# A feed-forward inner tile turned by VectorE in 32x32 blocks and put in order through DRAM, where TensorE turned it

## What is computed

```python
D_FF = ((8 * D_MODEL // 3 + 255) // 256) * 256     # 5632

def swiglu_ffn(x, norm_pre, w_gate, w_up, w_down, norm_post):
    h = rms_norm(x, norm_pre)
    a = jax.nn.silu(jnp.einsum('bsd,df->bsf', h, w_gate)) * jnp.einsum('bsd,df->bsf', h, w_up)
    y = jnp.einsum('bsf,fd->bsd', a, w_down)
    return x + rms_norm(y, norm_post)
```

## Time and profile before

| | us |
|---|---|
| median of 3 runs (lowest, highest) | 2074.62 (2074.54, 2075.27) |
| the profiled execution's own time | 2073.36 |
| its span | 2071.6 |
| TensorE busy within the span | 2033.2 |
| VectorE, ScalarE, GpSimd busy | 1181.7, 987.6, 197.6 |
| mean granted TensorE clock | 0.994 |

### The profile page before, as it was taken

How to read it: one execution, slowest core, us unless ns; L and a number is a source line. 1 busy time by engine, 2 the same in 40 slices (tenths; PEclk the granted TensorE clock), 3 DMA queues, 4 the chain that set the end, 5 groups by cost and what they waited for, 6 DMA issues and landing times.

```text
span 2071.6 us, 28886 instructions
## 1 busy us (share of the span) xinstructions
PE 2033.2 (98%) x10074; PEld 1724.3 (83%) x10074; DVE 1181.7 (57%) x1449; ACT 987.6 (48%) x1165; POOL 197.6 (10%) x118
## 2 busy tenths in 40 slices
PE   8999999999999999999999979999999999999998
PEld 6798888888888888888899968888888888888886
DVE  5745565555555544444599996565555555544444
ACT  5544464544455443433744475454444444443433
POOL 0000000000000000000688640000000000000000
PEclk9999999999999999999999989999999999999999
DMA  7735565555555555555355415565555555555554
GB/s 242 252 128 188 176 213 190 188 188 192 191 186 190 187 188 194 193 194 193 136 187 182 159 62 168 167 217 190 192 189 187 191 185 190 192 189 193 194 194 144
DMA packets 105128, 382.31 MB, mean 185 GB/s; under 512 B 11682, under 2 KB 12066, under 8 KB 104546
## 3 DMA queue, kind: packets, MB, share of 16 engines
q1 hardware_dynamic: 103968, 375.58, 54.3%
q0 software_dynamic: 944, 5.51, 0.8%
q10 hardware_dynamic: 148, 0.27, 0.1%
HBM read 379.21 MB, written 2.10 MB: 184 GB/s over the span
## 4 chain that ended last, share of the span: by engine, by line
PE 88%; DVE 8%; issue 3%; ACT 1%; DMA 1%; DVEq 0%; POOL 0%; SPq 0%; ACTq 0%
PE acc L1163 81%; DVE acc L1070 5%; PE acc L1174 1%; PE acc L1176 1%; PE acc L1175 1%; PE acc L1355 1%; DVE taps_now L1051 1%; PE acc L1213 0%; PE acc L1215 0%; DVE w_lo L785 0%; DMA vecs<-in_vecs 0%; DMA raw<-in_units 0%; ACT w_hi L463 0%; DVE conv L1072 0%; DVE acc L1065 0%
## 5 line engine op out<-in xcount | busy, mean ns | idle before, releaser
L785 DVE SCALAR_TENSOR_TENSOR w_lo<-raw,vecs,w_hi 128x1024 fp32r<-128x1024 f32 x400 | 512.7, 1284 | 474.7 <-ACT w_hi L463 472.7
L463 ACT ACTIVATE w_hi<-raw,vecs 128x1024 fp32r<-128x1024 f32 x400 | 459.9, 1153 | 525.1 <-PE acc L1163 491.4
L463 ACT ACTIVATE w_hi<-raw 128x1024 fp32r<-128x1024 f32 x304 | 322.7, 1064 | 460.5 <-PE acc L1163 358.5
L1163 PE MATMUL acc<-w_hi,xT_hi 128*128 128x512 f32 x1536 | 477.7, 392 | 5.3 <-DVE w_lo L785 4.7
L783 DVE TENSOR_TENSOR w_lo<-raw,w_hi 128x1024 fp32r<-128x1024 f32 x236 | 289.0, 1225 | 325.8 <-ACT w_hi L463 325.8
L1163 PE MATMUL acc<-w_lo,xT_hi 128*128 128x512 f32 x1536 | 473.8, 390 | 0.0
L1163 PE MATMUL acc<-w_hi,xT_lo 128*128 128x512 f32 x1536 | 473.3, 389 | 0.0
L1163 PEld LDWEIGHTS acc<-w_hi,xT_hi 128*128 128x128 f32 x1536 | 285.3, 188 | 66.9 <-issue 4.9
L1163 PEld LDWEIGHTS acc<-w_lo,xT_hi 128*128 128x128 f32 x1536 | 288.6, 188 | 60.5
L1163 PEld LDWEIGHTS acc<-w_hi,xT_lo 128*128 128x128 f32 x1536 | 288.6, 188 | 60.5
L1163 PE MATMUL acc<-w_hi,hT_hi 128*128 128x512 f32 x704 | 217.7, 389 | 0.0
(11 more groups left out here) (155 smaller groups left out, 1504.1 us busy)
## 6 DMA issues: line engine op xcount, KB each, us to landing
raw<-in_units SPq DMA_DIRECT2D x708, 512.0 KB, 3.3
gpost<-in_post POOLq DMA_DIRECT2D x4, 1024.0 KB, 6.1
x<-in_x SPq DMA_DIRECT2D x4, 512.0 KB, 8.0
out<-x SPq DMA_DIRECT2D x8, 256.0 KB, 2.8
tok<-in_lng POOLq DMA_DIRECT2D x1, 512.0 KB, 6.7
tok<-in_lnb POOLq DMA_DIRECT2D x1, 512.0 KB, 7.4
bs<-in_bs POOLq DMA_DIRECT2D x1, 256.0 KB, 7.9
taps<-in_taps ACTq DMA_DIRECT2D x1, 248.0 KB, 2.7
```

Source lines behind the costliest of these rows:

```text
L463: nc.scalar.activation(out, raw[:, s, :], ACT.Copy, scale=scale).then_inc(hi_ready, 1)
L785: ins = nc.vector.scalar_tensor_tensor(out[:, s, :], raw[:, s, :], vecs[:, gain:gain + 1], hi[:, s, :], ALU.mult, ALU.subtract)
L1163: last = mm(acc[:, 4 * par + 2 * t + h, :], xs, ws[:, s, h * BANK:(h + 1) * BANK], start=start and ws is w_hi and xs is xh, stop=stop and ...
```

## The change

Inner tiles are no longer turned by TensorE. After `hidden`, VectorE turns each token tile's 128x512 result in 32x32 blocks, from one half of the `tok` row to the other (`turn_hidden`, now VectorE's). SyncE stores it to a DRAM tensor (256 KB, one store per token tile, `store_hidden`) and, one quad later in its queue, fetches it back into the first half in an order that makes it usable as a stationary operand: four DMAs per token tile, one for each quarter of the partitions, 64 KB each, in runs of 512 bytes (`fetch_hidden`). The rows of the down weights are permuted on the host to match. `hi_hid` and `lo_hid` now read `tok` in place of PSUM and stand one quad later in their queues. SyncE's loop over quads is written out as a loop over inner tiles, so that the stores and fetches can stand between the loads. TensorE gets one wait per inner tile (for `hidden` of the previous inner tile) ahead of the fourth quad.

The core of the diff, in the order of the program: the views of the data, SyncE, ScalarE, VectorE, TensorE, the host. The same moves stand in the part of each engine that handles the last inner tile; they are left out here for ScalarE and VectorE.

```diff
+        def fetched(t):
+
+            return tok[:, t * DA:t * DA + BANK].rearrange("p (i k b) -> p k i b", k=4, b=32)
+
+        def by_token(hT, i, t):
+
+            return hT[:, bass.ts(i, 4), t * P:(t + 1) * P].rearrange("p k (i b) -> p k i b", b=32)
...
+            def store_hidden(i, layer):
+
+                for t in range(T):
+                    sp.wait_ge(hid_turned[t], i + (FFC * layer + 1))
+                    sp.dma_start(d_hid[t], tok[:, t * DA + BANK:(t + 1) * DA]).then_inc(hid_stored[t], 16)
+
+            def fetch_hidden(i, layer):
+
+                for t in range(T):
+                    sp.wait_ge(hid_stored[t], i * 16 + (FFC * layer + 1) * 16)
+                    src = d_hid[t].rearrange("(i a) (q n) -> q a i n", a=32, n=P)
+                    for quadrant in range(4):
+                        dst = tok[32 * quadrant:32 * (quadrant + 1), t * DA:t * DA + BANK].rearrange("p (i n) -> p i n", n=P)
+                        sp.dma_start(dst, src[quadrant]).then_inc(hid_fetched[t], 16)
+
+            def load_ffn(layer, q0):
+                pool = layer == 1
+                with sp.Fori(1, FFC) as i:
+                    load_quad(i * 4 + q0, pool)
+                    load_quad(i * 4 + (q0 + 1), pool)
+                    store_hidden(i - 1, layer)
+                    load_quad(i * 4 + (q0 + 2), pool)
+                    fetch_hidden(i - 1, layer)
+                    load_quad(i * 4 + (q0 + 3), pool)
+                qd = q0 + Q_FF
+                load_quad(qd, pool)
+                load_quad(qd + 1, pool)
+                store_hidden(FFC - 1, layer)
+                load_quad(qd + 2, pool)
+                fetch_hidden(FFC - 1, layer)
+
+            load_quads(1, Q_F0 + 4, lo_ready, lo_count)
+            load_ffn(0, Q_F0)
+            load_quads(Q_F0 + Q_FF + 3, Q_POOL0 + 1, lo_ready, lo_count)
+            load_quads(Q_POOL0 + 1, Q_POOL1 + 1, lo_ready_pool, lo_pool_count)
+            load_quads(Q_POOL1 + 1, Q_F1 + 4, lo_ready, lambda q, s: lo_count(q, s, True))
+            load_ffn(1, Q_F1)
+            load_quads(Q_F1 + Q_FF + 3, Q_END, lo_ready, lambda q, s: lo_count(q, s, True))
             for t in range(T):
...
-                def hi_hid(i, bank_par, t):
-                    act.wait_ge(hid_turned, i * 2 + (22 * layer + t + 1))
-                    nc.scalar.activation(hT_hi[:, bass.ts(i, 4), t * P:(t + 1) * P], pairs(4 * bank_par + 2 * t),
-                                         ACT.Copy).then_inc(hT_hi_ready, 1)
+                def hi_hid(i, t):
+                    act.wait_ge(hid_fetched[t], i * 64 + (FFC * layer + 1) * 64)
+                    nc.scalar.activation(by_token(hT_hi, i, t), fetched(t), ACT.Copy).then_inc(hT_hi_ready, 1)
 
                 def chunk(i, bank_par):
 
@@ -623,9 +670,9 @@
                     silu(i - 1, bank_par, 0)
                     silu(i - 1, bank_par, 1)
                     split_quad(i * 4 + (q0 + 1), gain, 4)
-                    hi_hid(i - 1, bank_par, 0)
-                    hi_hid(i - 1, bank_par, 1)
                     split_quad(i * 4 + (q0 + 2), gain, 8)
+                    hi_hid(i - 1, 0)
+                    hi_hid(i - 1, 1)
                     split_quad(i * 4 + (q0 + 3), gain, 12)
...
-                def lo_hid(i, bank_par, t):
+                def turn_hidden(i, t):
+                    dve.wait_ge(hid_ready, i * 2 + (22 * layer + t + 1))
+                    nc.vector.transpose(tok[:, t * DA + BANK:(t + 1) * DA],
+                                        tok[:, t * DA:t * DA + BANK]).then_inc(hid_turned[t], 1)
+
+                def lo_hid(i, t):
                     dve.wait_ge(hT_hi_ready, i * 2 + (22 * layer + t + 1))
-                    nc.vector.tensor_tensor(hT_lo[:, bass.ts(i, 4), t * P:(t + 1) * P], pairs(4 * bank_par + 2 * t),
-                                            hT_hi[:, bass.ts(i, 4), t * P:(t + 1) * P], ALU.subtract).then_inc(hT_lo_ready, 1)
+                    nc.vector.tensor_tensor(by_token(hT_lo, i, t), fetched(t), by_token(hT_hi, i, t),
+                                            ALU.subtract).then_inc(hT_lo_ready, 1)
 
                 def chunk(i, bank_par):
                     split_quad(i * 4 + q0, gain, 0)
                     hidden(i - 1, bank_par, 0)
                     hidden(i - 1, bank_par, 1)
+                    turn_hidden(i - 1, 0)
+                    turn_hidden(i - 1, 1)
                     split_quad(i * 4 + (q0 + 1), gain, 4)
-                    lo_hid(i - 1, bank_par, 0)
-                    lo_hid(i - 1, bank_par, 1)
                     split_quad(i * 4 + (q0 + 2), gain, 8)
+                    lo_hid(i - 1, 0)
+                    lo_hid(i - 1, 1)
                     split_quad(i * 4 + (q0 + 3), gain, 12)
...
-                def turn_hidden(i, bank_par):
-                    for t in range(T):
-                        pe.wait_ge(hid_ready, i * 2 + (22 * layer + t + 1))
-                        for n in range(4):
-                            last = nc.tensor.transpose(pairs(4 * bank_par + 2 * t)[:, n, :],
-                                                       tok[:, t * DA + n * P:t * DA + (n + 1) * P], ident[:])
-                        last.then_inc(hid_turned, 1)
-
                 def chunk(i, bank_par):
 
 
                     for c in range(4):
                         quad(i * 4 + (q0 + c), xT_hi, xT_lo, 4 * c, bank_par, start=c == 0,
                              stop=gu0_ready if c == 3 else None, after_pool=pool)
-                        if c == 0:
-                            turn_hidden(i - 1, 1 - bank_par)
+                        if c == 2:
+                            pe.wait_ge(hid_ready, i * 2 + 22 * layer)
...
-                        if j == 0 and c == 0:
-                            turn_hidden(FFC - 1, par)
...
-        return [gate_up.reshape(-1, P, UNIT), by_k(f_w_down[i], UNIT).reshape(-1, P, UNIT)]
+        down = f_w_down[i].reshape(FFC, 4, 4, 32, D).transpose(0, 2, 1, 3, 4).reshape(DFF, D)
+        return [gate_up.reshape(-1, P, UNIT), by_k(down, UNIT).reshape(-1, P, UNIT)]
```

More of the change, by code:

```diff
@@ L130, in lo_pool_count, with trunk @@
     return (q - Q_POOL0) * 4 + (s + 1)
-def trunk(nc, d_x, d_units, d_vecs, d_taps, d_ident, d_bs, d_lng, d_lnb, d_bpw2, d_post, d_out):
+def trunk(nc, d_x, d_units, d_vecs, d_taps, d_ident, d_bs, d_lng, d_lnb, d_bpw2, d_post, d_hid, d_out):
     with ExitStack() as ctx:
@@ L272, in trunk @@
         hid_ready = sem("hid_ready")
-        hid_turned = sem("hid_turned")
+        hid_turned = [sem(f"hid_turned{t}") for t in range(T)]
+        hid_stored = [sem(f"hid_stored{t}") for t in range(T)]
+        hid_fetched = [sem(f"hid_fetched{t}") for t in range(T)]
         hT_hi_ready = sem("hT_hi_ready")
@@ L343, in _, with load_quads, load_quad @@
             load_x(1, 1)
-            with sp.Fori(1, Q_POOL0 + 1) as q:
+            def load_quads(first, end, ready, count):
+                with sp.Fori(first, end) as q:
+                    for s in range(4):
+                        sp.wait_ge(ready, count(q - 1, s))
+                        load(q, s)
+            def load_quad(q, after_pool):
                 for s in range(4):
-                    sp.wait_ge(lo_ready, lo_count(q - 1, s))
+                    sp.wait_ge(lo_ready, lo_count(q - 1, s, after_pool))
@@ L638, in ffn @@
                 split_quad(qd + 1)
-                hi_hid(FFC - 1, par, 0)
-                hi_hid(FFC - 1, par, 1)
-                with act.Fori(qd + 2, qd + Q_DOWN // 2 + 1) as q:
+                split_quad(qd + 2)
+                hi_hid(FFC - 1, 0)
+                hi_hid(FFC - 1, 1)
+                with act.Fori(qd + 3, qd + Q_DOWN // 2 + 1) as q:
                     split_quad(q)
@@ L1004, in ffn @@
                 hidden(FFC - 1, par, 1)
+                turn_hidden(FFC - 1, 0)
+                turn_hidden(FFC - 1, 1)
                 split_quad(qd + 1)
-                lo_hid(FFC - 1, par, 0)
-                lo_hid(FFC - 1, par, 1)
-                with dve.Fori(qd + 2, qd + Q_DOWN // 2 + 1) as q:
+                split_quad(qd + 2)
+                lo_hid(FFC - 1, 0)
+                lo_hid(FFC - 1, 1)
+                with dve.Fori(qd + 3, qd + Q_DOWN // 2 + 1) as q:
                     split_quad(q)
@@ L1529 @@
     out = nc.dram_tensor("out", (SEQ, D), F32, kind="ExternalOutput").ap()
-    trunk(nc, *args, out)
+    hid = nc.dram_tensor("hid_turned_blocks", (T, P, BANK), F32, kind="Internal").ap()
+    trunk(nc, *args, hid, out)
     r = run_bass_kernel_spmd(nc, [{"in_" + n: v for n, v in arrays.items()}], core_ids=[0])
```

## The result

| | before | after |
|---|---|---|
| median, us (lowest to highest, 4 runs each) | 2074.94 (2074.54 to 2075.31) | 2055.34 (2054.57 to 2056.14) |
| the profiled execution's own time | 2073.36 | 2054.57 |
| its span | 2071.6 | 2052.8 |
| TensorE busy | 2033.2 | 2017.1 |
| VectorE busy | 1181.7 | 1205.1 |

The ratio is 0.9904, with a 95% interval of 0.9889 to 0.992. The prediction was 2055.4 us, 0.9907.

What follows compares the result with a forecast made beforehand. TensorE alone was taken to bound the feed-forward blocks. Removing its transposes saves 22 x 0.875 = 19.25 us and all additions cost nothing, so 2074.62 - 19.25 = 2055.4 us, range 2053 to 2060.

Steps and rivals of the forecast that it cites:

- What bounds the kernel: Feed-forward blocks: TensorE is busy all the time, so a nanosecond of TensorE is a nanosecond of the kernel.
- The price of a transpose: TensorE's chain: eight transposes per inner tile cost 0.875 us, 0.109 each; removing them saves 19.25 us.
- the rival that took the record's 272 ns: TensorE's transposes each cost their record's 272 ns on the chain, giving 2026.7 us; chance 0.03.
- VectorE's transposes: VectorE after `hidden`: two 128x512 transposes per inner tile, 0.7 us each, cost nothing, covered by TensorE's first quad.
- The point from which they would cost: VectorE's transposes delay TensorE only if they take over 2.4 us each.
- SyncE's queue: Stores and eight fetches between the loads: the next load goes 0.8 us late, at no cost.
- the bound of 2.5: Upper end, in us, of the delay of the load queued behind the eight fetches; still no cost.
- The fetch: Eight 64 KB fetches per inner tile, each landing in 1.9 to 8.0 us, at no cost to TensorE.
- The limit on the landing: Fourth quad's first unit: TensorE stalls only if the last fetch lands after 424.2, over 12.3 us from its issue.
- the axis: Time axis in us of one inner tile, on which the new work was placed; its first quad ends at 406.07.
- named as a risk: In the partly covered rival: DMA engines get busier and the loads' landing is a median; 2057.5 to 2070 us, chance 0.06.

Runs made afterwards that it cites:

- e1: The kernel before with only TensorE's eight transposes per inner tile left out, no VectorE transpose, store or fetch added: 2055.46 us, ratio 0.9908.
- e2: The kernel before with each of TensorE's transposes issued twice into the same place, 176 more: 2094.8 us, ratio 1.0097.
- e5: The changed kernel with each VectorE transpose done five times, one after the other: 2102.47 us, ratio 1.0131.
- e4: The changed kernel with each VectorE transpose done three times, one after the other: 2055.62 us, ratio 0.9906.
- e7: The changed kernel with fetches right behind the stores in SyncE's queue and the high and low copies one quad earlier: 2055.4 us, ratio 0.9909.
- e6: The changed kernel with the fetches behind the fourth quad's loads in SyncE's queue, the copies left in place: 2090.76 us, ratio 1.0074.
- e3: The changed kernel with TensorE's eight transposes per inner tile put back, their results read by nobody: 2074.9 us, ratio 1.0001.

## Why the prediction was right

*What bounds the kernel.* TensorE alone in the blocks; e1 shows it, since removing its work and nothing else gives the whole gain.

*The price of a transpose.* 0.109 us from the chain, confirmed by e1 (0.109) and e2 (0.114); the rival that took the record's 272 ns would have given 2026.7 and 2122.8 where 2055.3 and 2094.8 were measured. The term was a little small: layer 0's block took 708.97 us before (281.85 to 990.82) and 699.07 after, layer 1's 708.30 and 698.40, so 9.90 us each or 0.90 per inner tile, where the prediction had 0.875. That makes 19.8 us and not 19.25. The Trainium skill (TensorE: Matmul & The Clock Gate, Part 4: PE-mode transpose) has some 275 ns for bf16 data; here that is near the length of a record (272 ns, float32) and not the cost.

*VectorE's transposes.* Taken at 0.7 us, measured 0.684 (mean of the group 0.685). The point from which they would cost was put at 2.4 us each, 4.9 for the two, in what e5 shows to be the worst sort of inner tile: e4, with 4.2 us of them per inner tile, is free; e5, with 7.0, is not.

*SyncE's queue.* The eight issues took 3.66 us instead of 3.2 (0.43 for an issue, where a load's takes 0.33), so the next load went 1.7 us late instead of 0.8. It was covered, as the bound of 2.5 had been; e7 delays a load further and is free as well.

*The fetch.* 2.7 us to land, inside the 1.9 to 8.0 taken. The limit on the landing, 424.2 on the axis, is borne out by e6: 425.5 costs 1.5 us per inner tile.

*What was left out.* The loads' landing rose from 3.3 to 4.2 us, which I named as a risk and not in the sum; the copies take 0.615 instead of 0.585 us. Neither reaches TensorE.

*The rest, and luck.* That the median came within 0.1 us of the prediction is luck: the interval of the ratio is some 3 us to either side, and single executions of the same kernel differ by up to 3.5 us (2073.48 to 2076.95 for the kernel before). The profiled execution's span fell by 18.8 us and not by 19.8, since the chain reaches the first block 0.5 us later than before (282.34 against 281.85) and takes 0.6 us more between the blocks. In the stretch of 50 to 100 us the granted clock is 1.00 in the kernel before and in e3, 0.97 in the changed kernel, e1, e2, e4 and e7, and 0.93 in e5 and e6; it follows neither the change nor any one edit. No run tells what decides it.

## What to carry to other kernels

Price an instruction on a saturated TensorE by the distance that a run of them takes in the chain and never by the length of its record: here that is 0.11 against 0.272 us. Work moved off such an engine is free as long as each queue that it enters keeps its lead, and the leads can be read beforehand by putting one period on a time axis: for every moved instruction, when it is reached, what stands behind it, and when the bound engine wants that. Look whether all periods are alike before multiplying by their number: here five of 22 had a table load in them that made the lead 0.8 us shorter. What matters is not when the moved result is needed but what is queued behind the instruction that waits for it.

## What the runs showed of the hardware that I had not expected

After six gaps in an otherwise full TensorE that delayed it by 2.2 to 2.3 us (five in e5, one in e6), matmuls ran at the 1.2 GHz level five times, seven or eight of them at 0.43 us; after the 38 gaps of 0.8 to 1.9 us in the same two kernels it never happened. The one of e6, with 2.02 us of idle time ahead of it in the records:

```profile
702.50:709.20 6.70, 4.68 (x14) 3.46 (x13) 5.63 (x6) 4.17 (x5) 0.00 (x0) 0.75 0.46 142
```

A DMA's issue on SyncE's queue took 0.33 us for 128 runs of 4 KB or of 2 KB, 0.43 for 128 of 512 bytes in a 32x4 shape, and 0.38 for 16384 of 4 bytes. But behind one of the last sort the next issue took 13.4 us and more, and held up every load behind it. What sets the pace there is open.
